# Weighing a stage's first tile inside the stage before it, with its table loaded early and one transfer moved ahead of two others

## What is computed

```
def latent_layer(x, c, ...):
    h = rmsnorm(x, g_pre_l) * (1.0 + scale) + shift
    aq, ak, ..., dq, dzf, dzb, di, dg = split_branches(h, w_in_l)
    o_a = window_attn(...)
    o_b = neighborhood_attn(...)
    o_c, _ = retention_branch(...)
    o_d, _ = hgrn2_branch(dq, dzf, dzb, di, lb_l, st_d[:, 0], st_d[:, 1])
    return finish(x, (o_a, o_b, o_c, o_d), (ag, bg, cg, dg), w_out_l, g_post_l, gate)
```

## Time and profile before

| | us |
|---|---|
| median of 3 runs | 4110.41 (4109.98 to 4110.67) |
| profiled execution, its own time | 4101.01 |
| its span in the trace | 4099.2 |
| PE busy | 3822.4 (93%) |
| DVE busy | 2404.3 (59%) |
| ACT busy | 1202.8 (29%) |
| POOL busy | 572.4 (14%) |

### The profile page before, as it was taken

How to read it: one execution, slowest core, us unless ns; L and a number is a source line. 1 busy time by engine, 2 the same in 40 slices (tenths; PEclk the granted TensorE clock), 3 DMA queues, 4 the chain that set the end, 5 groups by cost and what they waited for, 6 DMA issues and landing times. The chain is left out here.

```text
span 4099.2 us, 63547 instructions
## 1 busy us (share of the span) xinstructions
PE 3822.4 (93%) x24448; PEld 2066.5 (50%) x24448; DVE 2404.3 (59%) x4838; ACT 1202.8 (29%) x3401; POOL 572.4 (14%) x870
## 2 busy tenths in 40 slices
PE   5999999999998997799999999999999989969997
PEld 3444555555554455455544445554555445545554
DVE  3223345324666887799942333551256688878996
ACT  2401232233331122344443023232333211224443
POOL 2000000100000354011000000001000005520000
PEclk7999999999999998899999999999999999979999
DMA  7432121232223334223333021213222233342222
GB/s 232 128 132 97 54 68 50 71 100 65 83 84 97 118 104 149 78 96 114 116 111 95 39 94 50 72 42 116 75 75 76 84 101 124 101 140 100 100 94 69
DMA packets 247772, 388.91 MB, mean 95 GB/s; under 512 B 42736, under 2 KB 163440, under 8 KB 247344
## 3 DMA queue, kind: packets, MB, share of 16 engines
q1 hardware_dynamic: 207504, 262.55, 20.5%
q0 software_dynamic: 39968, 122.30, 8.2%
HBM read 264.42 MB, written 122.25 MB: 94 GB/s over the span
## 5 line engine op out<-in xcount | busy, mean ns | idle before, releaser
L1160 PE MATMUL ps<-w_sb,hT 128*128 128x512 f32 x4608 | 2199.7, 611 | 3.7 <-ACT hT L1638 2.4
L1160 PEld LDWEIGHTS ps<-w_sb,hT 128*128 128x128 f32 x4608 | 815.4, 192 | 766.0 <-issue 727.2
L1510 PE MATMUL ps<-wo_sb,mT 128*128 128x512 f32 x1152 | 535.5, 609 | 50.6 <-ACT mT L1806 50.6
L979 POOL DMA_DIRECT2D projected<-row_t x252 | 138.2, 548 | 2472.7 <-DVE row_t L2014 1086.0
L2011 DVE RECIPROCAL e_t<-e_t 128x256 f32<-128x256 f32 (+1 forms) x180 | 430.8, 2393 | 6.2
L1510 PEld LDWEIGHTS ps<-wo_sb,mT 128*128 128x128 f32 x1152 | 210.8, 192 | 284.4 <-issue 213.6
L2009 DVE TENSOR_SCALAR e_t<-e_t 128x256 f32<-128x256 f32 (+1 forms) x180 | 71.2, 395 | 238.6 <-ACT row_t L1656 207.8
L1650 ACT ACTIVATE row_t<-ps 128x512 f32<-128x512 f32 x108 | 64.5, 597 | 392.7 <-PE ps L1160 350.0
L2111 DVE TENSOR_REDUCE nei_st<-ps 128x2 f32<-128x512 f32 x72 | 49.8, 691 | 205.7 <-PE ps L1269 205.7
L2144 DVE COPY win_pT<-ps 128x512 f32<-128x512 f32 x64 | 44.3, 692 | 213.4 <-PE ps L1278 213.4
L2144 DVE COPY nei_pT<-ps 128x512 f32<-128x512 f32 x64 | 44.3, 692 | 207.7 <-PE ps L1278 207.7
(11 more groups left out here) (243 smaller groups left out, 5391.7 us busy)
## 6 DMA issues: line engine op xcount, KB each, us to landing
projected<-row_t POOLq DMA_DIRECT2D x288, 256.0 KB, 2.8
w_sb<-in_w_in SPq DMA_DIRECT2D x14, 2048.0 KB, 9.3
wa<-in_w_ada SPq DMA_DIRECT2D x16, 1536.0 KB, 7.7
hg_raw<-projected SPq DMA_DIRECT2D x72, 256.0 KB, 4.2
out_streams<-y_t POOLq DMA_DIRECT2D x36, 512.0 KB, 4.2
hg_braw<-projected SPq DMA_DIRECT2D x108, 128.0 KB, 2.4
hg_raw<-projected SPq DMA_DIRECT2D x36, 384.0 KB, 3.9
mx_t<-mixed SPq DMA_DIRECT2D x36, 384.0 KB, 4.7
```

What stands on the lines that cost most here:

```text
L979: pool.dma_start(rows[tok(t), g * GRP:(g + 1) * GRP], row_t[:, p.slot]).then_inc(row_stored[p.slot], 16)
L1160: mm = nc.tensor.matmul(ps[:, p.bank, :], hT[:, k, t * P:(t + 1) * P], w_sb[:, g % 2, k, :], start=(k == 0), stop=(k == KC - 1))
L1510: mm = nc.tensor.matmul(ps[:, 6 + g, :], mT[:, t % 2, k, :], wo_sb[:, k, g * GRP:(g + 1) * GRP], start=(k == 0), stop=(k == KC - 1))
```

## The change

Six edits in the functions of the five engines:
1. **Table.** `keep` is moved to memory that the projections' input leaves free after `REST_END`, and is loaded in slot 33 with `past`, behind tile 0's keys.
2. **DVE.** Tile 0's levels 0 and 1 are computed in slot 34 (before: 0 to 2 in slot 35), levels 2 to 6 and the edges in slot 35 (before: 3 and 4 in slot 36, 5, 6 and edges in slot 37). The masks of heads 0 and 1 are applied at the end of slot 37, ahead of tile 1's level 0.
3. **PE.** `turn_hg(1)` is issued in slot 35, `weights(0, 0)` (64 small products) in slot 36, with the waits that they need. The stage begins at n = 1, and its wait for `hg.bs_ready` is at n = 2.
4. **ACT.** The banks of tile 1 are taken in slot 35, `weights_out` of heads 0 and 1 are at the end of slot 37. ACT and DVE also wait for `ret.out_ready` (POOL's last gating) ahead of the stage.
5. **POOL.** `keys_hg(0)` is issued in slot 35 instead of behind slot 37.
6. **SP.** In each iteration `mx_t` is loaded ahead of `load_hg_keys(n + 2)` instead of behind it.

```diff
@@ -324,7 +324,7 @@
 TURN_BANKS, O_BANK = (0, 1), 2
 
 HT_END = KC * NT * P
-HG_CORE = 14 * GW + P + 2 * P + 4 * GW + 4 + 12 * P + 16 * P + 8 * LEVELS * P + 8 * P + 4 * P + 128
+HG_CORE = 14 * GW + P + 2 * P + 4 * GW + 4 + 12 * P + 16 * P + 8 * LEVELS * P + 8 * P + 4 * P + 128 + (SLOTS + 1) * 64
 
 
 def count_turns():
@@ -497,6 +497,7 @@
         hg.qx = sb(s, "hg_qx", [P, 2, 2, 2, P])
         hg.ks = sb(s, "hg_ks", [P, 2, 2, P])
         hg.tc = sb(s, "hg_tc", [P, 2, 64])
+        keep = sb(s, "keep", [P, SLOTS + 1, 64])
...
@@ -506,7 +507,6 @@
         mT = sb(s, "mT", [P, 2, KC, P])
         y_t = sb(s, "y_t", [P, 2, D_MODEL])
         y_sq = sb(s, "y_sq", [P, D_MODEL], BF16)
-        keep = sb(s, "keep", [P, SLOTS + 1, 64])
         gp_sb = sb(s, "gp_sb", [P, 2, D_MODEL])
         hg.out_t = sb(s, "hg_out_t", [P, 2, GW])
         hg.o_c = sb(s, "hg_o_c", [P, 2, GW])
@@ -894,8 +894,9 @@
                 if m == REST_END:
                     last = PIECES[(l,) + PROJ_ORDER["rest"][-1]]
                     sp.wait_ge(proj_done, last.n + 1)
+                    load_hg_keys(0)
                     sp.dma_start(past[:, :], cols("after")).then_inc(hg.tab_in, 16)
-                    load_hg_keys(0)
+                    sp.dma_start(keep[:, :, :].rearrange("p s n -> p (s n)"), cols("keep")).then_inc(hg.tab_in, 16)
                     load_hg_keys(1)
                     load_hg_values(0)
                     load_hg_values(1)
@@ -912,19 +913,18 @@
                 sp.wait_ge(a.bk_ready, (l + 1) * NT)
                 sp.wait_ge(a.bs_ready, (l + 1) * NT)
             sp.wait_ge(ret.centred, (l + 1) * NT)
-            sp.dma_start(keep[:, :, :].rearrange("p s n -> p (s n)"), cols("keep")).then_inc(hg.tab_in, 16)
             for c in range(2):
                 sp.dma_start(gp_sb[:, c], gate_row[2 * l + c:2 * l + c + 1, :].broadcast_to([P, D_MODEL])).then_inc(wo_in, 16)
 
             for n in range(NT + 2):
-                if n + 2 < NT:
-                    load_hg_keys(n + 2)
                 t = n - 1
                 if 0 <= t < NT:
                     if t >= 2:
                         sp.wait_ge(bank_turned, TURNS[l, "own", t - 2] + 1)
                     sp.wait_ge(ret.stored[t % 2], 16 * (l * NP + t // 2 + 1))
                     sp.dma_start(mx_t[:, t % 2], mixed[tok(t), 0:3 * GW]).then_inc(mx_in[t % 2], 16)
+                if n + 2 < NT:
+                    load_hg_keys(n + 2)
                 t = n - 2
                 if 0 <= t < NT:
                     if t >= 2:
@@ -1101,10 +1101,11 @@
                     rope_ret(m - FORE + 2)
                 if 0 <= m - FORE - 2 < NT:
                     gate_ret(m - FORE - 2)
+                if m == REST_END + 2:
+                    keys_hg(0)
                 if m == REST_END + 1:
                     clear_decays(0)
                     clear_decays(1)
-            keys_hg(0)
             pool.wait_ge(ret.sf_ready, (l + 1) * NT)
             save_states(ret, ret.sf, out_ret, 0)
             pool.wait_ge(ret.bs_ready, (l + 1) * NT)
@@ -1538,21 +1539,24 @@
                     turn_ret(j + 1)
                 fill(2 * (more and m > 0))
                 if m == REST_END + 1:
-                    pe.wait_ge(hg.tab_in, 32 * l + 16)
+                    pe.wait_ge(hg.tab_in, 32 * (l + 1))
                     for n in (1, 2):
                         bank_out(pe, PIECES[PIECES[l, 0, 0].n + NG * NT - n])
                     turn_hg(0)
+                if m == REST_END + 2:
+                    turn_hg(1)
+                if m == BACK_SLOTS - 2:
+                    for done in (ret.p_ready, ret.sf_ready, ret.centred):
+                        pe.wait_ge(done, (l + 1) * NT)
+                    weights(0, 0)
                 if 0 <= j + 1 < NT:
                     scores_ret(j + 1)
                 fill(2 * (more and m > 0))
-
-            for a in (ret, hg):
-                pe.wait_ge(a.bs_ready, (l + 1) * NT)
-            for done in (ret.xT_ready, ret.p_ready, ret.sf_ready, ret.centred):
-                pe.wait_ge(done, (l + 1) * NT)
-            pe.wait_ge(hg.tab_in, 32 * (l + 1))
-            for n in range(NT + 2):
+            pe.wait_ge(ret.bs_ready, (l + 1) * NT)
+            pe.wait_ge(ret.xT_ready, (l + 1) * NT)
+            for n in range(1, NT + 2):
                 if n == 2:
+                    pe.wait_ge(hg.bs_ready, (l + 1) * NT)
                     pe.wait_ge(wo_in, 48 * (l + 1))
                 dense = project_out(n - 2) if n >= 2 else iter(())
 
@@ -1563,7 +1567,7 @@
                 if n >= 2:
                     turn_mixed(n - 2)
                 fill(3)
-                if 1 <= n <= NT:
+                if 2 <= n <= NT:
                     weights(n - 1, 0)
                 fill(5)
                 if 1 <= n <= NT:
@@ -1855,20 +1859,24 @@
                     square(j)
                 if REST_AT[m] and REST_AT[m][0] == 6:
                     bounds_ln(*REST_AT[m])
-                if m == REST_END + 1:
-                    take_decays(0)
-                    take_x(0)
-                    take_keys(0)
+                if m in (REST_END + 1, REST_END + 2):
+                    take_decays(m - REST_END - 1)
+                    take_x(m - REST_END - 1)
+                    take_keys(m - REST_END - 1)
+                if m == BACK_SLOTS - 1:
+                    act.wait_ge(ret.bs_ready, (l + 1) * NT)
+                    weights_out(0, 0)
+                    weights_out(0, 1)
 
             act.wait_ge(hg.bs_ready, (l + 1) * NT)
-            for used in (ret.kf_ready, ret.kv_done, ret.p_done, ret.qd_ready, ret.o_done, ret.centred):
+            for used in (ret.kf_ready, ret.kv_done, ret.p_done, ret.qd_ready, ret.o_done, ret.centred, ret.out_ready):
                 act.wait_ge(used, (l + 1) * NT)
-            for n in range(NT + 2):
+            for n in range(1, NT + 2):
                 if n >= 2:
                     take_mixed(n - 2, "mixed", 0)
                     squares(n - 2)
                     norm_stats(hg, n - 2)
-                if 1 <= n <= NT:
+                if 2 <= n <= NT:
                     weights_out(n - 1, 0)
                     weights_out(n - 1, 1)
                 if n >= 2:
@@ -2418,26 +2426,26 @@
                     scaled_ret(j - 1)
                 if piece and piece[0] == 6:
                     bounds_end(*piece)
+                if m == REST_END + 1:
+                    nc.vector.memset(hg.sf[:, 0, :], 0.0).then_inc(hg.clear, 1)
+                    for lv in range(0, 2):
+                        level_hg(0, lv)
                 if m == REST_END + 2:
-                    nc.vector.memset(hg.sf[:, 0, :], 0.0).then_inc(hg.clear, 1)
-                    for lv in range(0, 3):
-                        level_hg(0, lv)
-                if m == REST_END + 3:
-                    for lv in range(3, 5):
-                        level_hg(0, lv)
-                if m == REST_END + 4:
-                    for lv in range(5, LEVELS):
+                    for lv in range(2, LEVELS):
                         level_hg(0, lv)
                     edges_hg(0)
+                if m == BACK_SLOTS - 1:
+                    dve.wait_ge(hg.tab_in, 32 * (l + 1))
+                    masked_hg(0, 0)
+                    masked_hg(0, 1)
             dve.wait_ge(hg.clear, l + 1)
             dve.wait_ge(hg.s_in, 32 * (l + 1))
-            dve.wait_ge(hg.tab_in, 32 * (l + 1))
-            for used in (ret.p_done, ret.o_done, ret.kv_done, ret.kf_ready):
+            for used in (ret.p_done, ret.o_done, ret.kv_done, ret.kf_ready, ret.out_ready):
                 dve.wait_ge(used, (l + 1) * NT)
             for n in range(NT + 2):
                 if 1 <= n < NT:
                     level_hg(n, 0)
-                if 1 <= n <= NT:
+                if 2 <= n <= NT:
                     masked_hg(n - 1, 0)
                     masked_hg(n - 1, 1)
                 if n >= 2:
```

## The result

The changed kernel takes 4086.61 us in the median of 4 runs (4084.68 to 4088.38), the kernel before 4110.19 (4109.39 to 4110.67) beside it. The ratio is 0.9945, 95% interval 0.9932 to 0.9957. That is 23.6 us less; 29.5 was forecast, 4080.9, and the range was 4074 to 4092.

What follows compares the result with a forecast made beforehand. PE, busy 93% of the span, was taken as the bound, so only its stands or slow stretches could yield time. Terms of 9.6, 17.1 and 2.8 sum to 29.5 us: 4110.4 - 29.5 = 4080.9, range 4074 to 4092.

Steps and rivals of the forecast that it cites:

- `mx_t` ahead of the keys: Tile 1 of the last stage: PE's whole wait for this transfer goes, 8.33 and 8.78 us, 17.1 in all.
- The wait for DVE's masks of tile 2: Tile behind the first projection: DVE starts these masks 1.4 us late, so PE waits 0.8 us.
- The clock: Without the `mx_t` gap the following tile loses its cold stretch: 1.1 us in layer 1, 1.7 in layer 0, 2.8 in all.
- Terms 2 and 3: Last stage's early tiles: the `mx_t` wait removed (17.1 us) and the cold stretch behind it removed (2.8 us).
- The start: Last stage's start: tile 0's levels and masks done in the slots, gaining 4.8 us per layer, 9.6 for both.
- Slot 35 up to the end of `ret_out_t` lasted 5.87 us, PE's outputs in it: Duration read from the kernel before and reused in the changed kernel, making the stretch end at 3619.5.
- PE's half clock stays as it is: Stage's start: PE remains at half clock as before; its gaps between 3621 and 3646 get shorter but do not go.
- its 4.7: Stage's start, second half: PE's second masked weights follow DVE's masks by 1.15 us, at 3646.1, 4.7 us gained.
- the band that had 70%: Whole kernel: both stalls go, 24 to 36 us won, a time of 4074.4 to 4086.4 us.
- the first rival: Whole kernel: hand-overs at the start give the 9.6 us back, leaving 19.9 won, 4090.5 us; 13%.
- only the transfer pays: Stage's start: late `hg.bs_ready` delays next keys, values and masks, so the 9.6 us is lost; 4090.5 us, 13%.
- the fourth rival: Steady tiles: POOL's products stall DVE, which becomes the bound; two more 1.4 us stalls cost 47 us, giving 4128; 5%.

Runs made afterwards that it cites:

- e1: Kernel before with only the `mx_t` transfer moved ahead of the keys on SP; median 4086.06 us, ratio 0.9955.
- e5: Kernel before with only POOL's store of `hg_sf` moved behind `keys_hg(2)` and the ones of tile 3; median 4081.96 us.
- e4: Changed kernel with POOL's store of `hg_sf` moved behind `keys_hg(2)` and the ones of tile 3; ratio to the kernel before 0.9941.
- e10: Kernel before with only `keep` moved in memory, loaded in slot 33 and waited for by PE in slot 34; ratio 0.9992.
- e8: Changed kernel with 16 unread identity matmuls at the end of slot 34, where PE stands for `ret_p`; median 4079.39 us.
- e12: e11 with unread identity matmuls in three places: 28 ahead of `weights(0, 0)`, 14 and 8 ahead of tile 0's `hg_p` uses; median 4069.8 us.
- e11: Changed kernel with DVE's last-tile `ret_p` ahead of tile 0's levels and POOL's `hg_sf` store behind the ones of tile 3; median 4074.85 us.
- e13: e12 with 5 matmuls for 8, and first-iteration `gp_sb` load, tile 1's levels 1 to 3 and ACT's tile 2 keys later; median 4069.01 us.
- e9: Changed kernel with the edits of e3 and e4, and POOL's `keys_hg(0)` back behind slot 37; ratio to the kernel before 0.9926.
- e3: Changed kernel with DVE's `ret_p` of the last tile ahead of tile 0's levels, level 0 directly behind it; median 4075.28 us.

## Why the forecast was right in sign and 6 us too large

- **`mx_t` ahead of the keys (17.1)**: right. The wait went whole, 8.33 and 8.78, and both e1 and e5, which take it away in two different ways, confirm its cause. The wait for DVE's masks of tile 2 that was to come in its place came, as 24.94 us for the tile in place of 23.85: 1.09 measured where 0.8 was worked out; e4 takes it away by the cause that was named, POOL's ones behind the store.
- **The clock (2.8)**: 1.42 and 0.79 gained in the tile behind the wait, 2.2 (24.94 for it, 24.65 forecast). In the tile with the wait, which was to take what it took without its wait, layer 0 did (27.33 and 27.24), but in layer 1 it was 25.79 and is 26.96, 1.2 more. (The two layers were not alike within fractions of a us here, as the prediction has it: 36.11 and 34.12 with the wait.) The granted clock and PE's busy time show it, here in before's window from the first transpose to that of tile 1 (0.85 with the 8.33 us stand in it, 24.11 us busy), above in the changed kernel's (0.87, 25.27 us busy). More of the tile's work was done at half clock:

```profile
3652.90:3687.02 34.12, 24.11 (x214) 13.50 (x212) 23.04 (x51) 9.13 (x34) 5.08 (x8) 0.85 0.16 48
```

  Terms 2 and 3 were to give 19.9, and 18.2 came (10.29 and 7.95).
- **The start (9.6)**: this is the term that fell short, 5.3 came (3.1 and 2.2). The steps hold up to `ret_p` of tile 17, 16.20 us behind the mark where 4.9 more than 10.96, 15.86, was forecast, and again from the masks on (PE follows `hg_tc` by 1.16 and 1.07, forecast 1.15). Between them stands "Slot 35 up to the end of `ret_out_t` lasted 5.87 us, PE's outputs in it". That row was taken from a kernel in which PE had stood 0.41 us before the outputs. The change itself made it stand 5.64, the outputs ran at half clock, and the same stretch took 7.69, 1.8 more. The sentence that PE's half clock stays as it is looked at 3621 to 3646 only. In the second half the four levels of tile 1 took 8.02 us (3632.47 to 3640.49) where 7.5 was put in; the first of them alone took 2.99 with POOL's `hg_kd` and `hg_ks` beside it. 1.8, 0.3 and 0.5 are, to 0.1, the 2.5 us by which PE's second use of `hg_p` in layer 1 missed its 4.7 (it gained 53.10 - 50.89 = 2.2).
- **What the start's gain is made of** was read wrongly too. I set the wait for `keep` aside as DVE's work under another name, since the load is issued behind `hg.bs_ready`. But 3.1 us lie between the two (3626.8 and 3629.89), and `turn_hg(1)`, ACT's copies and 4.09 us of DVE's idle time (4.04 in layer 0) stand behind the load. e10 gives all of it with the load alone.
- **The range**: 4086.61 lies 0.2 us outside the band that had 70% (to 4086.4) and inside the range by the width that the first rival gave it. The band was also added up wrongly: the terms' own bounds, with 3 lost or 1 more, give 20.9 and 32.7 us, not 24 and 36.
- **The rivals**: "only the transfer pays" named hand-overs in the start that eat the gain, and about half of it went that way. Steady tiles are 23.85 us in all kernels, so no stall on the shared ports was added there (what the fourth rival had left per tile, 1.24 us, sets DVE's busy time of a 24 us window against a tile of 23.85; within the window it is 1.38); in slot 34 the 2.25 us row shows one where it was priced, 1.8 over the usual 0.43 where 1.4 was put in. This agrees with the Trainium skill ("SBUF — State Buffer", the section on the two separate sides) in that DVE is held beside POOL. That the later one waits the rows do not show: DVE's instruction starts 0.48 us ahead of POOL's first (3605.30 and 3605.78) and is the one that lasts long.
- The Trainium skill ("TensorE: Matmul & The Clock Gate", the section on HAM oscillation) says that each long idle gap is followed by a stretch at half rate. The trace agrees, and in the direction that the forecast left out: the new gap of 5.64 us brought its own stretch (granted clock 0.50), 1.8 us in what DVE waits for, and e8 removes most of it by filling the gap. The length of a gap alone does not tell what follows: behind 1.80 us in the kernel before (3614.01) PE's backward sums (`hg_braw,after`) took 1.19 us, against 0.60 in e12 at full clock, while behind 1.89 us in e8, after the filling, the outputs began at full clock (0.66).

## What to carry to other kernels

Before work is moved ahead of a hand-over between engines, ask how long the other engine will then stand, and price its next instructions at half clock too (here 1.12 us in place of 0.66 per group), and not only by the row of the kernel before. Compare the busy time of the engine that sets the stage's start over the same stretch in two kernels: where it is equal, only its idle time was won or lost, and the cheapest edit (here one load) may win as much as moving the work. When one wait has two conditions, take the time between the two as a gain of its own: here `hg.bs_ready` came 3 us ahead of the table, and loading the table early gave these 3 us, although nothing made `hg.bs_ready` earlier.

## What the runs showed of the hardware that I had not expected

- Matmuls that nobody reads made a kernel faster: 16 of 128x128 (0.24 us each at full clock) in a stand of 5.6 us gained 5.6 us over two layers in the traces, and 50 in three stands of e12 gained 4.9 more than e11 without them (41.0 and 36.1). The medians go the same way, with intervals of the ratios that overlap.
- How long the half clock lasts behind a stand varies. In the kernels in which the tile with the first projection begins at half clock (its first four records take 1.11 or 1.12 us, 0.66 in e12 and e13) and nothing in it is waited for at length, it took 25.71 to 27.24 us, though no edit touches PE's work in it. What sets its time stays open. In e12, where it begins at full clock, it took 23.89 in layer 0, a steady tile's time, and 25.54 in layer 1.
- The same code ahead of the change reached layer 0's mark between 1602.33 and 1611.67 us in the profiled executions. In the first 200 us the granted clock was 0.92 in the earliest (e9) and 0.87 in the changed kernel (1610.93), but 0.92 also in e3, which came at 1609.72; so this clock alone does not explain the spread.
